# Moving late conditioning pieces of a decoder trunk from the attention heads to the output projection

## The reference

```python
cond = jax.nn.silu(c)                                     # (1, 1024)
for l in range(DEPTH):                                    # DEPTH = 2
    mod = (cond @ w_ada[l] + b_ada[l])[:, None, :]        # (1, 1, 6144)
    shift1, scale1, gate1, shift2, scale2, gate2 = jnp.split(mod, 6, axis=-1)
    h = _rms_norm(x) * (1 + scale1) + shift1
    x = x + gate1 * _token_mixer(h, ...)                  # ends in y @ w_out[l]
    h = _rms_norm(x) * (1 + scale2) + shift2
    x = x + gate2 * _moe(h, ...)
return _rms_norm(x, final_gain)
```

## Time and profile before

| | |
|---|---|
| median of 3 runs | 2402.7 us (2392.19 to 2404.55) |
| the profiled execution | 2380.7 us, span 2378.7 us |
| mean granted TensorE clock | 0.928 |
| busy share of the span: TensorE, VectorE, ScalarE, GpSimd | 87%, 78%, 57%, 18% |
| heads of layer one and two, in the trace | 158.8 to 277.9 us, 1309.4 to 1424.7 us |
| output projection of layer one and two | 277.9 to 327.2 us, 1424.7 to 1474.0 us |

### The profile page before, as it was taken

The page is one execution under the profiler, slowest core; times in us unless marked ns, Lnnn a source line. Parts: engine busy times, 40 slices in busy tenths (PEclk is TensorE's granted clock), DMA queues, the critical chain, the costliest instruction groups (busy, mean ns, idle before and its releaser), DMA issues. The chain is left out here.

```text
span 2378.7 us, 37805 instructions
## 1 busy us (share of the span) xinstructions
PE 2062.4 (87%) x10000; PEld 1645.0 (69%) x10001; DVE 1848.3 (78%) x2424; ACT 1355.7 (57%) x1724; POOL 437.9 (18%) x345
## 2 busy tenths in 40 slices
PE   2889988999999999995079898999999999999960
PEld 0655576888888888884046456778888888888850
DVE  5656645999999999995773773589999889999957
ACT  2323422777777877873122352267777777877741
POOL 0200300122113222222020021012222232222210
PEclk9997999999999999998569889999999999999985
DMA  7035123899899999994742531379999989899847
GB/s 277 22 120 182 67 94 148 304 359 353 337 354 346 348 350 353 349 354 183 287 155 67 182 119 39 148 272 349 348 347 346 346 335 351 332 355 362 329 152 278
DMA packets 134953, 618.44 MB, mean 260 GB/s; under 512 B 22612, under 2 KB 25684, under 8 KB 81768
## 3 DMA queue, kind: packets, MB, share of 16 engines
q1 hardware_dynamic: 112232, 550.52, 61.4%
q0 software_dynamic: 22656, 67.13, 7.9%
HBM read 581.68 MB, written 43.65 MB: 263 GB/s over the span
## 5 line engine op out<-in xcount | busy, mean ns | idle before, releaser
L1361 DVE TENSOR_TENSOR w_lod<-raw_d,w_hid 128x2048 fp32r<-128x2048 f32 x136 | 312.7, 2299 | 32.7 <-ACT w_hid L1174 23.1
L1119 POOL DMA_INDIRECT y_rows<-mixT,sidx x136 | 225.1, 1655 | 542.8 <-issue 446.3
L1358 DVE TENSOR_TENSOR w_loa<-raw_gu,w_hia 128x2048 fp32r<-128x2048 f32 x136 | 310.6, 2284 | 9.4 <-ACT w_hia L1172 8.4
L1358 DVE TENSOR_TENSOR w_lob<-raw_gu,w_hib 128x2048 fp32r<-128x2048 f32 x136 | 310.3, 2282 | 0.0
L1172 ACT ACTIVATE w_hia<-raw_gu 128x2048 fp32r<-128x2048 f32 x136 | 261.3, 1921 | 25.7 <-PE bank L1516 20.6
L1187 ACT ACTIVATE mixT<-bank 128x512 f32<-128x512 f32 x272 | 147.9, 596 | 206.8 <-PE bank L1516 205.4
L1105 POOL DMA_INDIRECT mixT<-h_rows,gidx x138 | 131.9, 956 | 710.0 <-issue 689.5
L1174 ACT ACTIVATE w_hid<-raw_d 128x2048 fp32r<-128x2048 f32 x136 | 261.1, 1920 | 0.0
L1172 ACT ACTIVATE w_hib<-raw_gu 128x2048 fp32r<-128x2048 f32 x136 | 259.2, 1906 | 0.0
L1366 DVE TENSOR_TENSOR hbT_lo<-bank,hbT_hi 128x512 fp32r<-128x512 f32 x272 | 175.2, 686 | 107.1 <-ACT hbT_hi L1180 107.1
L1514 PE MATMUL bank<-w_hid,actT_hi 128*128 128x512 f32 x544 | 227.7, 419 | 12.7 <-DVE actT_lo L1402 12.7
(11 more groups left out here) (332 smaller groups left out, 3869.3 us busy)
## 6 DMA issues: line engine op xcount, KB each, us to landing
raw_gu<-in_w_gate SPq DMA_DIRECT2D x136, 1024.0 KB, 5.0
raw_gu<-in_w_up SPq DMA_DIRECT2D x136, 1024.0 KB, 7.5
raw_d<-in_w_down SPq DMA_DIRECT2D x136, 1024.0 KB, 8.2
w_ada_sb<-in_w_ada SPq DMA_DIRECT2D x40, 1024.0 KB, 5.6
raw_gu<-y_rows SPq DMA_DIRECT2D x32, 1024.0 KB, 6.5
w_in_sb<-in_w_out SPq DMA_DIRECT2D x16, 512.0 KB, 7.0
w_in_sb<-in_w_in SPq DMA_DIRECT2D x2, 3072.0 KB, 22.8
hT<-in_w_ada SPq DMA_DIRECT2D x4, 1024.0 KB, 11.2
```

The lines of the kernel that those rows point to most:

```text
L1119: by_rows(s, lambda rows: pool.indirect_dma_start(out=y_dram, in_=yb[s.par][0:rows], in_offset=None, out_offset=bass.IndirectOffsetOnAxis( ...
L1358: dve.tensor_tensor(w_lo[k][:].rearrange("p c g f -> p g c f"), raw_gu[s.par][:, :, 4 * k:4 * k + 4, :], w_hi[k][:].bitcast(F32).rearrange ...
L1361: dve.tensor_tensor(w_lo[2][:], raw_d[s.par][:], w_hi[2][:].bitcast(F32), ALU.subtract).then_inc(lo[2], 1)
```

## The change

Pieces 8 to 11 (scale2 and gate2) move from the heads to the output projection. Pieces 4 to 7 stay in the heads and take two heads each.

```diff
@@ the places and the count of the units @@
-        ada_at = [w_ada[:, 0], w_ada[:, 1], hT[:, 0:4, :], hT[:, 4:8, :], mixT[:, 0:4, :], mixT[:, 4:8, :]]
+        LATE = 16
+        ada_at = [w_ada[:, 0], w_ada[:, 1], hT[:, 0:4, :], hT[:, 4:8, :], mixT[:, 0:4, :], mixT[:, 4:8, :],
+                  h[:].rearrange("p a (c n) -> p (a c) n", c=2), qk[:]]

         def ada_unit(u):

+            if u >= LATE:
+                return ada_at[AHEAD + u % 2], AHEAD + u % 2, 16 * ((u - LATE) // 2 + 1)
             n = u if u < AHEAD else u % 2
@@ SyncE @@
+                    if u >= LATE:
+                        sp.wait_ge(s_O, HEADS * TJ)
                     if u >= AHEAD:
                         sp.wait_ge(s_unit, u - 1 if u >= AHEAD + 2 else u - AHEAD + 1)
@@ ScalarE @@
-                        if i == 3 and hd >= 1:
-                            mod_out(3 + hd)
+                        if i == 3 and hd >= 2 and hd % 2 == 0:
+                            mod_out(3 + hd // 2)
...
-                mod_out(11)
+                mod_out(7)
...
+                mod_out(8)
                 for j in range(TJ):
+                    if j < 3:
+                        mod_out(9 + j)
                     act.wait_ge(s_x, TJ + j + 1)
-                    act.activation(h[:, 0, :], x[:, j, :], ACT.Square, accum_out=stat[:, 16 + j:17 + j]).then_inc(s_alink, 1)
+                    act.activation(latent[:, 0:2, :].rearrange("p a n -> p (a n)"), x[:, j, :], ACT.Square, accum_out=stat[:, 16 + j:17 + j]).then_inc(s_alink, 1)
@@ VectorE @@
-                        ada(4 + hd, (range(0, 3), range(3, 5), range(5, 8), ())[i])
+                        at = 4 * (hd % 2)
+                        ada(4 + hd // 2, (range(at, at + 1), range(at + 1, at + 2), range(at + 2, at + 4), ())[i])
...
                 dve.wait_ge(s_mod, 6)
+                ada(8, range(0, 4))
                 for b in range(2):
                     for j in range(TJ):
                         n = TJ * b + j
+                        if n < 7:
+                            ada(8 + (n + 1) // 2, range(4 * ((n + 1) % 2), 4 * ((n + 1) % 2) + 4))
                         dve.wait_ge(s_y, n + 1)
@@ TensorE @@
-                    if n % TJ == 2 and n >= TJ:
-                        ada(3 + n // TJ)
+                    if n % TJ == 2 and n >= 2 * TJ and n // TJ % 2 == 0:
+                        ada(3 + n // TJ // 2)
...
-                ada(3 + HEADS)
+                ada(7)
...
                 for j in range(TJ):
+                    ada(8 + j)
                     pe.wait_ge(s_x, j + 1)
                     mixed_out(1, j, range(DC)).then_inc(s_y, 1)
```

More of the change, by code:

```diff
@@ L344, in mixer @@
         s_in_hi, s_in_lo, s_hT_hi = sem("s_in_hi"), [sem("s_in_lo_keys"), sem("s_in_lo_rest")], sem("s_hT_hi")
-        d_ada = [sem(f"d_ada{n}") for n in range(AHEAD)]
+        d_ada = [sem(f"d_ada{n}") for n in range(AHEAD + 2)]
         d_row = [sem("d_row0"), sem("d_row1")]
@@ L406, in _ @@
                     ada(2 * q + 1)
-                    for m in range(2 * (q - 4), min(2 * (q - 4) + 2, DC)):
+                    for m in range(2 * (q - 4), 2 * (q - 4) + 2) if q < 8 else ():
                         sp.dma_start(w_out[:, m, :], dram("w_out", l).rearrange("o (m p) n -> m p (o n)", p=P)[m]).then_inc(d_out, 16)
@@ L918, in _ @@
                     else:
-                        pe.wait_ge(s_mod, 12)
+                        pe.wait_ge(s_mod, 8)
                     for m in range(4):
```

## The result

The changed kernel takes 2416.3 us (median of 20 runs, 2396.9 to 2428.2), the kernel before 2392.5 us (median of 20 runs, 2378.5 to 2411.0). The ratio is 1.0098, with a 95% interval of 1.0077 to 1.0119: slower by one per cent, +23.9 us. The profiled execution of the changed kernel took 2416.2 us, with a span of 2414.4 us and a mean granted clock of 0.919. That of before took 2380.7 us, near the lower end of its 20 runs, so the spans of the two profiles stand 35.7 us apart and not 24.

The account below looks back on a forecast made before the run. TensorE was taken to fill the projection, the heads to wait on VectorE's chain and slow-clock spells. Per layer 8.2 + 0.3 - 4.7 + 2.4 = +6.2 us, 12.4 for two; 2402.7 + 12.4 = 2415 us, range 2400 to 2428.

Parts of the forecast that it names:

- rival B: Heads: the clock falls at every head end, +10 to +12 us per layer, 2422 to 2427 us; chance 0.20.
- A: The forecast itself: slower by the projection, partly paid back in the heads, 2408 to 2422 us; chance 0.50.
- Products of the late pieces in the projection: Projection's second half: four pieces' products cost TensorE their length, 4 x 2.06 = +8.2 us per layer.
- VectorE in the projection: Projection: the last unit of the moved pieces is ready slightly late, +0.3 us per layer, 0 to about 4.
- near 58: Sign in the projection: the stage should take near 58 us, its second half stepping by 7.6 us per token block.
- VectorE in the heads: Heads: waits at step 1 go and the wait after head 6 shrinks, -4.7 us per layer, bounds -2.3 to -7.
- The clock in the heads: Heads: about one more spell at 1.2 GHz per layer, +2.4 us, bounds -2.4 to +8.
- The queues: Loads on SyncE, w_out loads and ScalarE's copies: nothing; without cover 1 to 3 us on SyncE, w_out at most 2.
- The prediction's own sign for B: Heads: a clock falling below 0.75 would show that it falls at every head end.
- C: Heads return all of the cost: step-1 waits vanish and a spell falls away, 2400 to 2407 us; chance 0.16.
- D: Heads: VectorE sets their pace, gain up to 24 us per layer, 2396 at half, 2372 in full; chance 0.09.
- E: Projection: the moved products are hidden there, 2399 us; chance 0.05.

Follow-up runs that it names:

- e1: The changed kernel with TensorE's products of pieces 8 to 11 cut from 512 to 16 columns; projection 61.4 and 60.7 us.
- e3: The changed kernel with unread products filling the ends of heads 0, 1, 3, 5 and 7; 2389.6 us, ratio 0.9987 to the kernel before.
- e10: e3 with all of piece 8's VectorE operations ahead of the split of the attention output; 2399.7 us against 2395.2, ratio 1.0018.
- e11: e10 with the late pieces' bias added in VectorE's first operation, one TensorE product instead of two; 2384.6 us, ratio 0.9958 to the kernel before.
- e2: The kernel before with the products of heads 1, 3, 5 and 7 cut from 512 to 16 columns; heads 123.5 and 128.0 us.
- e4: The kernel before with half of VectorE's conditioning operations in the heads left out; heads 114.3 and 115.9 us.
- e7: The kernel before with unread products filling the end of head 0; 2393.0 us against 2390.0, ratio 1.002.
- e9: The changed kernel with unread products at the ends of heads 1, 3, 5 and 7 but not 0; single run 2403.3 us.
- e8: The kernel before, head 0's end filled, VectorE's operations per head set 1, 2, 5 instead of 3, 2, 3; 2395.2 us against 2390.0, ratio 1.0037.
- e5: The changed kernel with three of VectorE's four operations in each unit of pieces 8 to 11 left out; projection 60.3 and 59.9 us.
- e6: The changed kernel with both the products and VectorE's operations of pieces 8 to 11 cut; projection 54.6 and 54.4 us.

## Why the prediction was right, and where its sizes were off

The forecast was 2415 us in a range of 2400 to 2428, with slower as the likeliest side; the measured time is 2416.3. The closeness is partly luck. The three runs of the kernel before that were shown had a median 10.2 us above that of 20 runs, and the forecast difference, +12.4 us, was half of the measured +23.9. Taken as a difference, the result stands where rival B was put, not in the middle of A. By steps:

- **Products of the late pieces in the projection**, +8.2 per layer. Right: they come every 7.65 us (forecast 7.6), so each costs 7.65 - 5.54 = 2.11, and the four 8.4. But e1 shows that VectorE's chain has the same length: "that is tight" in the prediction meant that cutting either gives next to nothing.
- **VectorE in the projection**, +0.3. Measured: the last piece comes 0.43 us late, one load is waited for 0.73 us (forecast 0.8). The loads land in 5.0 to 7.0 us, with medians of 5.1 and 5.8 for the two places. Right.
- **What the step on the projection lacked**: the clock at its start. Head 7 ends at 1.2 GHz, and the first passes run at 0.63 us until 280.2. The first half of the stage ends 303.35 - 275.77 = 27.6 us after its start, where it was 292.2 + 4 x 2.77 - 277.9 = 25.4: +2.2 us, in layer two +2.7. In e3, with the ends filled, this start is at full clock, and the stage takes 58.4 to 58.5, the "near 58" of the prediction.
- **VectorE in the heads**, -4.7. As mechanism right: gaps of 2.48 behind heads 1, 3 and 5, 0.37 behind 2 and 4, 0.63 before head 7; a head at full clock takes 11.58 us (the bound given was 11.8). Head 6 was to take 12.3 us at full clock; it takes 16.5. Of its 2.75 us of waiting 2.1 went (forecast 2.4), and a longer spell at 1.2 GHz came.
- **The clock in the heads**, +2.4, is the term that was mis-sized. It was worked out as one spell more per layer at 3 us or less. Measured are 9.0 us more of slow time in layer one and 18.1 in layer two; at the prediction's own price, 2.35 us for a spell of 6.8, that is 3.1 and 6.3 us. The bounds given, -2.4 to +8, do hold it: the heads came out at -2.1 and +3.3 where -4.7 and the clock's share add up, so, if the -4.7 is right, the clock took +2.6 and +8.0. The count of spells was also wrong at its start: it had five in the first layer, and there were six, since head 0 held one before its end was reached (its clock of 0.76 above). After the change head 0's is the shorter one, and heads 1, 6 and 7 hold the long ones. Layer two, which was counted like layer one, had been the better one before ("five and the second fewer") and lost most. As equal code moves by as much between layers and profiles, the difference between the two layers should be given no cause.
- **The queues**: nothing forecast, nothing found.

Of the rivals, **B** (clock at every emptied end) is the mechanism that e3, with e10 and e11, shows: filling the ends raises the clock with TensorE's work increased. e2 points the same way from the other side. The 0.20 that it was given looks low. Not every head fell, as B had it (heads 3 and 4 ran at full clock), but head 7 and the projection's start did. The prediction's own sign for B, a clock in the heads below 0.75, did not come: it was 0.76 and 0.77. The sign was set too low to tell B from A. **C** and **D** expected time back from VectorE's relief. e4 gives that by itself: 114.3 and 115.9 us, not the 100 or so of D in full. The relief is there, 7 to 18 us per layer, but only once no head end is empty (e7 to e3, e10 and e11), where the clock takes less of it. **E** (products hidden) is refuted for the change as a whole, but e1 shows its half truth: with VectorE as long as TensorE there, the products aren't alone in holding the stage.

The rule of the Trainium skill, page SBUF — State Buffer, section "two separate sides", that the prediction drew on found no case among the late pieces of the change, as forecast, but one in e10, where a piece was put over GpSimd's splits: 5.06 us instead of 2.33. The pieces in head 6 of the change met it as before: one operation took 1.57 us there and two took 2.58.

The Trainium skill, page TensorE: Matmul & The Clock Gate, section "What's actually happening", takes activity as what lifts the clock from its default. The table above agrees in its direction: in each column the kernel with the least work on TensorE has the most slow time, 37.5 against 71.5 us on the left (e7, e2, layer two) and 17.1 against 55.6 on the right (e3, after).

What stays open: how much a single end is worth. Filling head 0 alone gives nothing with VectorE's full share (e7), and with half of it the 10.5 and 13.0 us between e9 and e3 are about what equal code shows. In e7 head 0 takes 14.22 us at a clock of 0.76 with its end filled, so something ahead of that end decides there. It may be the wait at step 1: e8, which takes that wait out and keeps VectorE's full share, has its head 0 in 11.82 us at 0.86. But e10's layer one, without that wait too, starts with a spell as long as e7's, so this isn't shown. Open too is why equal code falls into more or fewer spells: e10 and e11, with the heads of e3, took 110.4 and 112.5 us in one of their layers, and e5, with the heads of the change, 112.8 in one and 126.0 in the other.

## What to carry to other kernels

Work that hides in another engine's wait may be holding up TensorE's clock: before it is moved away, look at the granted clock of that stretch and at the gap that will be left, and fill the gap with products if nothing better is at hand (here 2 us each, in gaps that were there anyway, and five to a layer, gave back 27 us between the medians of the change and of e3). When two engines have the same length in a stage, cutting one shows next to nothing, and only the pair of cuts does. Where equal code moves by 10 us between profiles, collect it from every kernel that holds it before a difference of that size is given a cause. And where the time before is known from few runs, forecast the difference; the absolute figure can be right by accident.

## What the runs showed of the hardware

- More work on TensorE made the same stage shorter: with ten more products in eight heads these took 101.2 to 112.5 us in six layers (e3, e10, e11), where without them they took 112.8 to 126.0 in eight (after, e1, e5, e6). The clock was 0.81 to 0.92 instead of 0.69 to 0.80.
- The granted clock doesn't repeat with the code: the same eight heads held 17.1 us at 1.2 GHz in e3 and 42.0 in e11's first layer, 44.5 and 77.2 in the two layers of e5.
- The level at which a stage ends is carried into the next: the projection's first passes took 0.63 us for 4.4 us after head 7 had run at 0.51, and 0.39 us at once in e3.
- A VectorE multiply-add over 128x512 took 0.75 us alone and 1.7 us beside GpSimd's splits (e10: 5.06 us for three). Of the next four, 5.80 us in all, the last ran at 0.75 us, after the splits had ended at 282.75.
